# Banded attention layer of a two-layer block on one Trainium2 core: the transposes of a unit's weights move from behind the quarter projection tile to a place in front of it

## The reference, cut to what matters

```python
def sliding_window_sink_attention(u, positions, w_qkv, sinks, w_o):
    qkv = u @ w_qkv
    q, k, v = jnp.split(qkv, ...)
    q = rotary(q, positions); k = rotary(k, positions)
    ...
        s = jnp.einsum('blkgd,bckd->bkglc', qb, kb) * scale
        s = jnp.where(valid, s, -jnp.inf)
        m = jnp.maximum(jnp.max(s, axis=-1), sink)
        p = jnp.exp(s - m[..., None])
        den = jnp.sum(p, axis=-1) + jnp.exp(sink - m)
        ob = jnp.einsum('bkglc,bckd->blkgd', p, vb) / den
    ...
    return out @ w_o
```

## Time and profile before

| what | value |
|---|---|
| median of three runs | 2508.92 us |
| the profiled execution | 2509.11 us |
| its span (first to last instruction) | 2507.3 us |
| TensorE matmul busy | 2387.8 us, 95% |
| VectorE busy | 1198.5 us, 48% |
| ScalarE busy | 1107.2 us, 44% |
| GpSimd busy | 1028.1 us, 41% |
| the stretch from the first scores to the last values of the banded layer | about 1810 to 1927 us |

### The profile page before, as it was taken

How to read it: one execution, slowest core, us unless ns; L and a number is a source line. 1 busy time by engine, 2 the same in 40 slices (tenths; PEclk the granted TensorE clock), 3 DMA queues, 4 the chain that set the end, 5 groups by cost and what they waited for, 6 DMA issues and landing times.

```text
span 2507.3 us, 40093 instructions
## 1 busy us (share of the span) xinstructions
PE 2387.8 (95%) x13062; PEld 1947.0 (78%) x13062; DVE 1198.5 (48%) x2375; ACT 1107.2 (44%) x2396; POOL 1028.1 (41%) x750
## 2 busy tenths in 40 slices
PE   7999999999999889998999999999898999999998
PEld 6787888787877668666878888888766878888886
DVE  4555555554677753575344622223785424522224
ACT  5433333345544545553644632323565634523232
POOL 4444444442533324441651444443422742544442
PEclk9999999999999989998999999999999999999999
DMA  5333333332322213221431232332322421332332
GB/s 188 112 98 98 96 99 95 105 102 85 110 85 84 84 51 92 65 79 53 128 111 47 93 99 94 92 99 77 93 64 81 136 92 51 101 101 93 97 92 79
DMA packets 126065, 231.99 MB, mean 93 GB/s; under 512 B 17120, under 2 KB 17248, under 8 KB 125920
## 3 DMA queue, kind: packets, MB, share of 16 engines
q1 hardware_dynamic: 123072, 219.56, 29.1%
q10 hardware_dynamic: 2848, 10.49, 1.2%
HBM read 208.48 MB, written 2.10 MB: 84 GB/s over the span
## 4 chain that ended last, share of the span: by engine, by line
issue 54%; PE 22%; POOL 22%; ACT 1%; POOLq 1%; DVE 1%; ACTq 0%; DMA 0%; DVEq 0%; SPq 0%
POOL wl L401 22%; PE PS L430 20%; PE PS L499 1%; PE PS L511 0%; POOLq L400 0%; PE PS L468 0%; POOLq L409 0%; ACT wh L1077 0%; PE PS L458 0%; PE PS L506 0%; ACTq L1087 0%; DMA raw<-tiles_dram 0%; ACT work L1106 0%; DVE ul L1697 0%; DVE ul L1706 0%
## 5 line engine op out<-in xcount | busy, mean ns | idle before, releaser
L401 POOL TENSOR_TENSOR wl<-raw,wh 128x512 fp32r<-128x512 f32 x746 | 1027.9, 1401 | 1451.6 <-ACT wh L1077 1450.3
L430 PE MATMUL PS<-uh,wh 128*128 128x512 f32 (+1 forms) x2120 | 798.6, 377 | 23.0 <-DVE ul L1706 8.6
L430 PE MATMUL PS<-uh,wl 128*128 128x512 f32 (+1 forms) x2120 | 782.4, 369 | 0.0
L430 PE MATMUL PS<-ul,wh 128*128 128x512 f32 (+1 forms) x2120 | 781.7, 369 | 0.0
L1077 ACT ACTIVATE wh<-raw 128x512 fp32r<-128x512 f32 x746 | 430.4, 623 | 349.7 <-PE PS L430 279.3
L430 PEld LDWEIGHTS PS<-uh,wh 128*128 128x128 f32 x2120 | 402.8, 190 | 111.1 <-issue 19.5
L430 PEld LDWEIGHTS PS<-uh,wl 128*128 128x128 f32 x2120 | 402.5, 190 | 67.6
L430 PEld LDWEIGHTS PS<-ul,wh 128*128 128x128 f32 x2120 | 403.1, 190 | 62.8 <-issue 0.8
L430 PE MATMUL PS<-wh,hid_sb 128*128 128x512 f32 x1024 | 322.0, 396 | 0.0
L1225 ACT ACTIVATE work<-PS 128x512 f32<-128x512 f32 (+1 forms) x156 | 89.7, 575 | 354.8 <-PE PS L430 281.4
L430 PEld LDWEIGHTS PS<-wh,hid_sb 128*128 128x128 f32 x1024 | 192.4, 188 | 46.2
(11 more groups left out here) (224 smaller groups left out, 2413.6 us busy)
## 6 DMA issues: line engine op xcount, KB each, us to landing
raw<-tiles_dram SPq DMA_DIRECT2D x746, 256.0 KB, 2.7
work<-work SPq DMA_DIRECT2D x296, 64.0 KB, 2.0
gB<-post_dram ACTq DMA_DIRECT2D x8, 512.0 KB, 3.7
H<-x_dram SPq DMA_DIRECT2D x4, 512.0 KB, 6.3
H<-x_dram ACTq DMA_DIRECT2D x4, 512.0 KB, 6.7
work<-mem_dram ACTq DMA_DIRECT2D x2, 1024.0 KB, 6.2
out_dram<-H ACTq DMA_DIRECT2D x4, 512.0 KB, 2.6
cst<-consts_dram SPq DMA_DIRECT2D x1, 644.0 KB, 5.1
```

The source lines that it names most:

```text
L401: nc.gpsimd.tensor_tensor(w_of(wl, slot)[:, hc], raw[:, s, hc], w_of(wh, slot)[:, hc].bitcast(F32), ALU.subtract).then_inc(lo_ready, 1)
L430: last = nc.tensor.matmul(out, a, b, start=start and m == 0, stop=stop and m == 2)
```

## The change

Two lines of `attend` change places. With `between` given, one turn now issues S(n+2), T(n), Q(n+1) (or B), V(n-1). Nothing is added or removed, no semaphore changes its meaning, and no other engine's list is touched. For the two attentions without `between` the order stays as it was.

```diff
@@ -836,9 +836,9 @@
                 for n, un in enumerate(units):
                     if n + 2 < len(units):
                         unit_scores(n + 2)
+                    transposes(U + n, PS[:, TB0 + n % 2, :], un["probs"], ahead=2)
                     if between is not None:
                         between(n)
-                    transposes(U + n, PS[:, TB0 + n % 2, :], un["probs"], ahead=2)
                     if n >= 1:
                         values(n - 1)
                 if between is not None:
```

## The result

The changed kernel took 2515.89 us (median of 7 runs, 2512.43 to 2519.01) against 2509.36 us (median of 7, 2507.97 to 2511.75) for the kernel before. The ratio is 1.0026 with a 95% interval of 1.0014 to 1.0037. A second series of five runs gave 2516.73 us against 2507.91 us, and a ratio of 1.0040 (1.0027 to 1.0053). Between the medians the change costs 6.5 us in the first series and 8.8 us in the second. The forecast was 2516.9 us. The profiled execution took 2517.43 us.

A forecast was written before the change was run, and what follows sets the result against it. TensorE, 95% busy, and VectorE were taken as nearly level in the edited stretch. Terms -0.2 + 2.7 + 0.2 + 5.1 = +7.8 on the profiled 2509.11 us gave 2516.9 us, range 2508 to 2522.

The forecast's parts named there:

- What bounds the kernel: Between 1810 and 1927 us TensorE and VectorE are nearly level; T waits five times for the scaling, 6.1 us in all.
- Step 1: Switches between TensorE operations: T to Q 0.35 us instead of 0.53, a gain of 0.18 us a turn.
- Steps 2 and 3: Q no longer covers T's wait for the scaling; from scaling 6 to S(10) 5.70 us instead of 4.57, +1.13.
- Step 4: GpSimd's subtractions meet the third unit's scaling on VectorE in every head: about 13.9 us a head.
- The sum without the clock: Four heads 56.2 against 53.48 us, +2.7; -0.2 ahead of unit 6, +0.2 from T(22) on: +2.7 us.
- Step 5: TensorE's clock falls behind three of five long T waits, 1.7 us each: +5.1 us, ends 0 and +8.5.
- A: The forecast: cover lost and the clock falls in some waits; 2516.9 us, 2512 to 2522; chance 0.50.
- B: Rival: cover lost but the clock holds; 2512 us, 2508 to 2515; chance 0.28.
- C: Rival: nothing visible, VectorE sets the pace and longer waits are only moved; 2509 us; chance 0.09.
- D: Rival: faster, GpSimd's subtractions end before the scaling starts in heads 1, 3 and 5; 2502.7 us; chance 0.06.
- E: Rival: all five waits lower the clock and S ahead of T costs 0.87 us; 2523 us; chance 0.07.
- The swap of the query halves: Swap of a query tile's halves, copied later; costed at nothing, with a cover of some 2 us before VectorE needs it.

The follow-up runs named there:

- one part alone: Against the kernel before, T ahead of Q only in the third unit of the first six heads: 2511.93 us; only in all other units: 2510.27 us.
- all waits filled: Changed kernel with 12 identity transposes ahead of the waits of T(6), T(10), T(14), T(18), T(22) and T(26): 2514.98 us, 1.0031 to the kernel before.
- `k % 4 == 3`: Next weight tile's high part made behind the fourth unit's copy: 2542.09 us in the changed kernel, 2529.90 us in the one with all other units moved.
- all other units moved: Kernel before with T ahead of Q in all units but the third of the first six heads: 2510.27 us, ratio 1.0008.

## Why the prediction was right, point by point

**What bounds the kernel.** Read rightly but for one wait: of the five waits of T, the one of 0.52 us is at T(23), and only the one of 0.88 us is at the end of the layer. Nothing hangs on it.

**Step 1, the switches.** Too cheap. I booked 0.35 us for T to Q, from a place where no wait stood between, and 1.50 for Q to V. Measured 0.41 and 1.57, so a turn is 3.21 and not 3.08 us: a gain of 0.04 us a turn in place of 0.17.

**Steps 2 and 3, the cover and who waits behind it.** Right in place and sign. From the end of scaling 6 to S(10) I had 5.70 us. With the scaling's end at 1837.53 and S(10) at 1843.47 it is 5.94, and the 0.24 more are step 1's error over two turns. Before it was 4.57.

**Step 4, GpSimd.** Right in kind, 0.45 us a head too cheap. I put GpSimd at 11.02 to 13.58 us behind scaling 6 and the end of scaling 10 at 13.9; the rows say 11.4 to 13.9, and 14.35. Of the 0.45 us, 0.35 is the later end of GpSimd, which is step 1's error carried through T(9). The other 0.1 is the second half of the scaling, which ended 0.42 us behind GpSimd and not 0.31. The low part of a finished head lengthened the last head by 0.2 us and not by 0.6. The count by the port's lock gave the shape: L2333 took 0.61 us and ended at 1850.25, when GpSimd's first subtraction did (1850.24), and the first half of L2338 ended 0.15 us behind the second (1851.61 and 1851.46). The Trainium skill, SBUF — State Buffer, section "SBUF: two separate sides", names besides the two-port modes "two SBUF inputs" against a GpSimd operation that reads SBUF. The runs agree: the products at L1796 and L1799 took 1.6 us instead of 0.69 as soon as GpSimd was moved onto them. What step 4 did not say, and the traces with one part alone do: the loss is not the sum of its parts. T ahead of Q in units 8 and 9 brings GpSimd forward; that lets it catch the scaling that T(10) now waits for without cover. With the cover kept, the same meeting in every head left the heads at 13.4 us.

**The sum without the clock.** I had +2.7 us. The four heads gave 57.4 - 53.5 = 3.9 instead of my 2.7, mostly step 1's error four times over. Behind T(22), where I booked +0.2, there were 0.7 us with all waits filled. Together that is 4.6 us from T(6) on. Ahead of T(6), where I booked -0.2, the profile shows +0.4, which may be spread.

**Step 5, the clock.** The term that was mis-sized. I had three falls at 1.7 us, +5.1. The profiled run had two, and they cost 2.4 us together: 1.5 us in the head that shows one by itself, and less behind T(22). In the medians the part is between nothing and 2 us. The fall behind a wait of 2.1 us is as uncertain as the earlier trace rows had it: two of five in each of two profiled runs.

So the total was right by luck, through two errors that cancel: about 2 us too little for the order itself, about 3 us too much for the clock. The mechanism of A is there in both its parts, the lost cover and falls in some waits, but it is divided wrongly: the lost cover, which B priced at 2.7 us, is the larger part with 4.6 us. C and D are out: VectorE's waits for scores rose from 1.9 to 11.4 us, and GpSimd, which had begun 0.83 us behind the small sum of a cheap head's scaling, now begins 0.67 us ahead of it and does not end ahead of it. E is out too: two falls and not five, and S ahead of T costs 0.63 us. The swap of the query halves, booked at nothing, held here: its cover was enough in the changed kernel. The two runs with `k % 4 == 3` show what the loss of that cover costs: about 25 us on the changed kernel, and about 20 on the one with all other units moved.

## What to carry to other kernels

Work that can run at any time belongs in front of the wait of an in-order queue, not behind it: behind it, it is added to the path of everything the queue releases next. Before an order is changed, look at which engine comes free earlier, and on what it then lands; here a copy made 1.5 us sooner brought GpSimd onto VectorE in every head instead of every second one. With the cover in place that cost nothing, without it about 1 us a head. So test the parts of such a change together as well as apart: in the traces two parts that cost 2.0 and 0.1 us alone cost 3.9 us together.

## What the hardware showed that I had not expected

Even a VectorE operation over two columns, 0.16 us alone, is held until GpSimd's subtraction ends (0.61 us), as a product of 512 columns is (1.6 us for 0.69); and both sides pay, for GpSimd's two subtractions took 2.97 us beside the product and 2.49 us beside the sum and scaling of the changed kernel. A VectorE operation that is held shows a longer duration and no idle time, so no list of waits names it. And the same wait can be followed by a low clock or not. Of the four waits of 2.1 us from T(6) to T(18) one was, in both profiled runs of the changed kernel, once behind T(10) and once behind T(14). The wait of 1.8 us at T(26) was followed by one in three other kernels' profiles and by none in these two.
